# Summing the squares of two pre-norms on the tensor engine, and all residual additions of the post-norms on the vector engine

## The reference, cut to what matters

```python
x = x + rms_norm(merged @ w_out[l], norm_mix_post_g[l])     # post-norm 1, residual 1
h = rms_norm(x, norm_ffn_pre_g[l])                          # needs mean(x*x) of residual 1
f = (silu(h @ w_gate[l]) * (h @ w_up[l])) @ w_down[l]
x = x + rms_norm(f, norm_ffn_post_g[l])                     # post-norm 2, residual 2
# second block, first line:
x = x + 0.5 * swiglu(rmsnorm(x, ffn1_norm[l]), ...)         # needs mean(x*x) of residual 2
```

## Time and profile before

| | |
|---|---|
| median of 3 runs | 2029.11 us (2029.0 to 2029.81) |
| profiled execution | 2032.4 us, its span 2030.3 us |
| PE busy | 1972.8 us, 97% |
| DVE busy | 992.5 us, 49% |
| ACT busy | 761.7 us, 38% |
| POOL busy | 281.7 us, 14% |
| mean granted TensorE clock | 0.986 |

### The profile page before, as it was taken

The page is one execution under the profiler, slowest core; times in us unless marked ns, Lnnn a source line. Parts: engine busy times, 40 slices in busy tenths (PEclk is TensorE's granted clock), DMA queues, the critical chain, the costliest instruction groups (busy, mean ns, idle before and its releaser), DMA issues.

```text
span 2030.3 us, 22840 instructions
## 1 busy us (share of the span) xinstructions
PE 1972.8 (97%) x9064; PEld 1599.2 (79%) x9064; DVE 992.5 (49%) x1502; ACT 761.7 (38%) x1150; POOL 281.7 (14%) x273
## 2 busy tenths in 40 slices
PE   8989999989999999899999999999999999999997
PEld 6767788868888887688888877777887788888886
DVE  6676634374334335633433465665654454334334
ACT  5344523353223234432322355565543343223223
POOL 5121001231011012310100120120110011011012
PEclk9999999999999999999999999999899999999998
DMA  5211233423333324233333231211232233333331
GB/s 159 83 52 53 63 89 94 119 77 101 103 94 94 103 79 119 75 103 93 96 102 94 85 101 44 63 52 53 63 98 68 60 96 104 94 103 95 94 88 57
DMA packets 343404, 175.72 MB, mean 87 GB/s; under 512 B 6306, under 2 KB 343299, under 8 KB 343299
## 3 DMA queue, kind: packets, MB, share of 16 engines
q1 hardware_dynamic: 343298, 174.27, 29.7%
HBM read 172.15 MB, written 2.10 MB: 86 GB/s over the span
## 4 chain that ended last, share of the span: by engine, by line
PE 89%; DVE 5%; issue 2%; POOL 2%; ACT 1%; DMA 0%; SPq 0%; DVEq 0%; POOLq 0%; ACTq 0%
PE ps L962 27%; PE ps L966 27%; PE ps L964 26%; PE ps L1012 1%; PE ps L1021 1%; PE ps L1029 1%; PE ps L1045 1%; POOL TS L1732 1%; PE ps L982 1%; PE ps L992 1%; PE ps L1090 1%; POOL X L1758 1%; PE ps L1108 1%; PE ps L975 1%; PE ps L1033 1%
## 5 line engine op out<-in xcount | busy, mean ns | idle before, releaser
L1371 DVE TENSOR_TENSOR WL<-RAW,WH 128x1024 fp32r<-128x1024 f32 (+2 forms) x336 | 401.9, 1199 | 709.9 <-ACT WH L1147 709.6
L962 PE MATMUL ps<-HH,WH 128*128 128x512 f32 x1728 | 687.9, 398 | 7.9 <-DVE TS L1404 6.0
L966 PE MATMUL ps<-HL,WH 128*128 128x512 f32 x1728 | 679.5, 393 | 12.6 <-DVE HL L1381 12.5
L964 PE MATMUL ps<-HH,WL 128*128 128x512 f32 x1728 | 678.6, 393 | 4.0 <-DVE WL L1371 4.0
L1147 ACT ACTIVATE WH<-RAW 128x1024 fp32r<-128x1024 f32 (+2 forms) x336 | 342.3, 1021 | 543.9 <-PE ps L966 535.6
L966 PEld LDWEIGHTS ps<-HL,WH 128*128 128x128 f32 x1728 | 327.3, 189 | 87.3 <-DVE HL L1381 18.7
L962 PEld LDWEIGHTS ps<-HH,WH 128*128 128x128 f32 x1728 | 327.8, 190 | 83.9 <-DVE TS L1404 8.4
L964 PEld LDWEIGHTS ps<-HH,WL 128*128 128x128 f32 x1728 | 328.0, 190 | 74.4 <-DVE WL L1371 6.6
L962 PE MATMUL ps<-GH,WH 128*128 128x512 f32 x720 | 282.0, 392 | 0.0
L966 PE MATMUL ps<-GL,WH 128*128 128x512 f32 x720 | 280.6, 390 | 0.0
L964 PE MATMUL ps<-GH,WL 128*128 128x512 f32 x720 | 280.2, 389 | 0.0
(11 more groups left out here) (196 smaller groups left out, 1523.5 us busy)
## 6 DMA issues: line engine op xcount, KB each, us to landing
RAW<-in_ffn_w_gu SPq DMA_DIRECT2D x88, 512.0 KB, 3.8
RAW<-in_w_in SPq DMA_DIRECT2D x68, 512.0 KB, 3.9
RAW<-in_ffn_w_down SPq DMA_DIRECT2D x32, 512.0 KB, 4.0
RAW<-in_w_gate SPq DMA_DIRECT2D x22, 512.0 KB, 3.8
RAW<-in_w_up SPq DMA_DIRECT2D x22, 512.0 KB, 3.8
RAW<-in_w_out SPq DMA_DIRECT2D x16, 512.0 KB, 4.0
RAW<-in_mem_w_kv SPq DMA_DIRECT2D x16, 512.0 KB, 3.9
RAW<-in_w_down SPq DMA_DIRECT2D x16, 512.0 KB, 4.0
```

Of the source, the lines that this page charges most:

```text
L962: e.matmul(bk, wh, xh, start=k == 0, stop=False)
L964: e.matmul(bk, wl, xh, start=False, stop=False)
L966: last = e.matmul(bk, wh, xl, start=False, stop=k == kt - 1)
L1371: e.tensor_tensor(m["WL"][:, s, 0:kt, :], m["RAW"][:, n % NRAW, 0:kt, :], m["WH"][:, s, 0:kt, :].bitcast(F32), ALU.subtract).then_inc(*sg. ...
```

## The change

For generations 1 and 2 (`SUMMED`), the squares are no longer added up chunk by chunk on POOL and DVE. Each square stays in its own tile, and PE multiplies it by `onesD` into one PSUM bank that accumulates over the eight chunks (`sum_square`, f32 operands). The matmul of chunk c stands in PE's order between the first pair's matmuls of chunk c and those of chunk c+1; that of chunk 7 follows the pair. `rstd` has no matmul of its own for these two norms. All eight additions to X in each post-norm run on DVE, each right behind the scaling of the same chunk; POOL's `post` is gone, and with it the second semaphore for X.

```diff
+SUMMED = (1, 2)
...
-def x_event(gen, c):
-    return ("xp" if gen in (1, 2) and c % 2 else "x", (gen, c))
...
     def feed(self, gen, c, gcol, free):
+        key = ("n", gen)
         self.step("feed", gen, c, gcol + c, free)
-        self.square(("n", gen), c, ("X", c), T, x_event(gen, c))
+        if gen in SUMMED:
+            self.tiles.take((key, c))
+            self.step("square", key, (key, c), ("X", c), T, ("x", (gen, c)))
+        else:
+            self.square(key, c, ("X", c), T, ("x", (gen, c)))
+
+    def sum_square(self, key, c):
+        if c == 0:
+            self.bank(("stat", key))
+        self.step("sum_square", key, c)
+        self.tiles.give((key, c), ("ssq", (key, c)) if c < KD - 1 else ("stat", key))
 
     def rstd(self, key, acc, ev, ones, eps, cols=T):
-        self.bank(("stat", key))
-        self.tiles.give(acc, ("stat", key))
+        if acc is not None:
+            self.bank(("stat", key))
+            self.tiles.give(acc, ("stat", key))
...
-                if n == f == 0:
+                if n == f == 0 and gen in SUMMED:
+                    sums = iter(range(-1, KD))
+
+                    def before():
+                        c = next(sums)
+                        if c >= 0:
+                            self.sum_square(("n", gen), c)
+
+                    mg, mu = self.mtiles([sg, su], ("H", gen, 0), [bg, bu], before=before)
+                    before()
+                elif n == f == 0:
                     mg, mu = self.mtiles([sg, su], ("H", gen, 0), [bg, bu])
...
 # tensor_program
+    def sum_square(key, c):
+        g.wait_ge(*sg.at("ones", 0))
+        g.wait_ge(*sg.at("sq", (key, c)))
+        if c == 0:
+            wait_all(at.bank_free(("stat", key)))
+        e.matmul(at.bank(("stat", key)), m["onesD"], at.tile((key, c)), start=c == 0, stop=c == KD - 1).then_inc(
+            *(sg.inc("ssq", (key, c)) if c < KD - 1 else sg.inc("stat", key)))
+
     def rstd(key, acc, ev, ones, eps, cols):
+        if acc is None:
+            return
...
 # vector_program, post
-        if c % 2 == 0:
-            g.wait_ge(*sg.at("post", (gen, c)))
-            g.wait_ge(*sg.at(*x_event(gen - 1, c)))
-            e.tensor_tensor(X[:, c, :], X[:, c, :], y, ALU.add).then_inc(*sg.inc("x", (gen, c)))
+        g.wait_ge(*sg.at("post", (gen, c)))
+        g.wait_ge(*sg.at("x", (gen - 1, c)))
+        e.tensor_tensor(X[:, c, :], X[:, c, :], y, ALU.add).then_inc(*sg.inc("x", (gen, c)))
...
 # pool_program
-    def post(gen, c, t, ev, gcol):
-        if c % 2:
-            X = m["X"][:, c, :]
-            g.wait_ge(*sg.at("post", (gen, c)))
-            g.wait_ge(*sg.at(*x_event(gen - 1, c)))
-            e.tensor_tensor(X, X, at.tile(t), ALU.add).then_inc(*sg.inc("xp", (gen, c)))
```

More of the change, by code:

```diff
@@ L199, in norm @@
             self.held[gen] = True
-            self.rstd(("n", gen), ("n", gen), ("acc_last", ("n", gen)), "onesD", 0)
+            self.rstd(("n", gen), None if gen in SUMMED else ("n", gen), ("acc_last", ("n", gen)), "onesD", 0)
         return ("n", gen)
@@ L388, in post_norm @@
             self.step("post", gen, c, t, ev, gcol + c)
-            self.tiles.give(t, x_event(gen, c))
+            self.tiles.give(t, ("x", (gen, c)))
             if c:
@@ L413, in evac @@
         def evac(mt, b, mm, part=0, last=True):
-            before = ("x", (gen, mt, part - 1)) if part else x_event(gen - 1, mt)
+            before = ("x", (gen, mt, part - 1)) if part else ("x", (gen - 1, mt))
             self.step("add_x", gen, mt, b, mm, scale, before, None if last else part)
@@ L1117, in finish @@
         o.then_inc(*sg.inc("fin", 0))
-    todo = dict(gain0=gain0, gain1=gain1, turn_x=turn_x, memory_turn=memory_turn, mm=mm, rstd=rstd, turn=turn, scores=scores,
+    todo = dict(gain0=gain0, gain1=gain1, turn_x=turn_x, memory_turn=memory_turn, mm=mm, sum_square=sum_square,
+                rstd=rstd, turn=turn, scores=scores,
                 turn_probs=turn_probs, values=values, stick_map=stick_map, stick_weights=stick_weights, level=level,
@@ L1149, in feed @@
     def feed(gen, c, gcol, free):
-        g.wait_ge(*sg.at(*x_event(gen, c)))
+        g.wait_ge(*sg.at("x", (gen, c)))
         g.wait_ge(*sg.at("gain", 0 if gen == 0 else 1))
@@ L1780, in store @@
             e.tensor_tensor(y, y, m["ST"][:, 0, 0:4].unsqueeze(2).to_broadcast([P, 4, P]), ALU.mult).then_inc(*sg.inc("op", c))
-    todo = dict(first_consts=first_consts, consts=consts, square_add=square_add, scores=scores, merge=merge, gate_r=gate_r, post=post,
+    todo = dict(first_consts=first_consts, consts=consts, square_add=square_add, scores=scores, merge=merge, gate_r=gate_r,
                 prepare=prepare, k_decay=k_decay, store=store)
```

## The result

Four runs of the changed kernel gave 2013.53 us in the median (2012.71 to 2015.99), beside 2029.05 us for the kernel before (2027.14 to 2029.81, four runs). The ratio is 0.9927, interval 0.991 to 0.9944. A second measurement, with more runs of the kernel before, gave 2016.64 us (2012.63 to 2019.16, six runs) beside 2028.9 us: 0.9938, interval 0.9926 to 0.995. The forecast was 2017.2 us.

What follows compares the result with a forecast made beforehand. PE's order of work sets the time, with DVE, slowed by POOL, the bound in both post-norm stages. Gains of 5.9 and 6.0 us sum to 11.9: profiled 2032.4 to 2020.5, less 3.3 gives 2017.2 us; 8-in-10 range 2013.0 to 2021.5.

Steps and rivals of the forecast that it cites:

- DVE is the bound before, because of POOL: In both post-norm stages DVE is busy 23.50 and 22.75 us; its additions take 1.66 us beside POOL, 0.69 alone.
- the 2.05 us per chunk that was worked out: DVE in the stages without POOL: scaling 0.78, addition 0.61 and `HL` 0.66 us for each chunk.
- the four waits for `HL`: PE in the old first stage waits at chunks 1, 3, 5 and 7; one 1.81 us wait stands for all four.
- 0.87 us per f32 matmul: PE's cost for each `sum_square` at full clock; 6.1 us more PE work per stage, 12.2 in all.
- PE is the bound after, at 2.23 us per chunk: New stages: PE needs 6 x 0.227 + 0.87 us per chunk against DVE's 2.05, so PE bounds by a small margin.
- The waits for squares, banks and tiles cost nothing, and the next `WL` is in time: New stages: squares, banks and tiles cost nothing; first stage's next `WL` is done at 436.1, before PE's 437.87.
- The clock stays up: PEclk 1.00 in both stages, with no PE wait of more than 1 us.
- B: Rival: in each stage the clock still falls once, costing 1.65 us; gain 8.6, 2020.5 us; chance 0.14.
- C: Rival: low clock for most of each stage makes the kernel slower, 2038 us in a middle case, 2050 at worst; chance 0.04.
- D: Rival: DVE's additions in the stages stay slow, 3.0 us per chunk, nothing gained, within 1 us of 2029; chance 0.04.
- A: Rival: `sum_square` costs PE only 0.46 us, DVE bounds the stages, gain 15.8, 2013.3 us; chance 0.08.
- the last one, taking the stages' gain from the profiled execution over to the median: Whole kernel: profiled 2032.4 us would become 2020.5; the median, 3.3 us below the profiled run, would be 2017.2.

Runs made afterwards that it cites:

- the reduced ones: Changed kernel with squares and the matrix of 1/1024 in reduced f32 format (fp32r) for the 16 sum matmuls: 2013.8 us, ratio 0.992.
- the run with the additions alone: Kernel before with all eight additions of each post-norm on DVE, squares still summed on POOL and DVE: 2026.5 us, ratio 0.9989.
- the run with waits of 0.4 us in every 2.05 us: Changed kernel with the eight f32 matmuls of each sum all behind the pair instead of between its chunks: 2024.59 us, ratio 0.9977.

## Why the prediction was right, step by step

- *DVE is the bound before, because of POOL.* Shown: POOL's additions alone, without consumers, make the stage 24.3 us; without POOL DVE runs at the 2.05 us per chunk that was worked out. One reading of the rows was too plain: of the four waits for `HL` (chunks 1, 3, 5 and 7) three were of one kind (1.81, 1.77 and 1.80 us), and the fourth was 0.30 us, behind one of 0.65 us for ACT's `HH`. It entered no term of the sum.
- *0.87 us per f32 matmul.* 0.86 us, by itself and doubled.
- *PE is the bound after, at 2.23 us per chunk.* 2.25 us: in the stage matmuls start every 0.23 us or a little more. Stage lengths were forecast as 19.6 and 18.8 us and are 19.74 and 18.96; the sum as 11.9 us and is 11.6.
- *The waits for squares, banks and tiles cost nothing, and the next `WL` is in time.* PE's timeline shows two waits, 0.31 and 0.40 us, both in chunk 0 and as forecast, then only the short wait and restart at chunk 1, 0.27 us together, as forecast.
- *The clock stays up.* 1.00 in both stages. Rivals B and C are out, D by the 0.69 us of all sixteen additions, A by the doubled matmuls.
- *The time.* 2017.2 us against 2013.5 and 2016.6. The step that was too plain is the last one, taking the stages' gain from the profiled execution over to the median as if nothing else moved. One run holds some 28 to 42 us at low clock outside the stages, which shifts it by several us either way. Of eleven runs of the changed kernel six lie between 2012.6 and 2014.4 and four at 2018.8 or above; the first four were on the low side, by luck.
- What stays open: the medians gave 15.5 and 12.3 us, the stages 11.6. Both intervals hold 11.6 (11.4 to 18.3 and 10.1 to 15.0 us by the ratios), and three profiles of each kernel show no order in the low time; whether one or two of the extra us are the change's doing, by when the mixers' waits come, was not settled.

The forecast did not say what either half of the change is worth; the experiments give nearly all of it to the sums.

## What to carry to other kernels

A helper engine's instruction costs not only its own queue: where POOL and DVE both read two tiles of SBUF, read the durations of the DVE instructions beside it, and price a POOL addition at the microsecond that it takes from a DVE with work to do. Work put on an engine that waits for another can cost little if it fills those waits chunk by chunk (by the estimate 8 x (0.87 - 0.23) the f32 sums are 5.1 us more work for PE than the reduced ones, and they make the stage 2.0 us longer), and costs much more when the same work stands at the end (4.1 us more). Compare kernels by the length of the stage that was changed, between the same two instructions; the whole time also holds how often the clock fell elsewhere.

## What the runs showed of the hardware that was not expected

- In the run with the additions alone, POOL's additions of two 128x512 tiles and DVE's instructions with two SBUF inputs took turns: POOL's ended 1.13 to 1.15 us behind the DVE instruction that it started beside, and the DVE instruction of 0.75 us that started next ended 0.54 to 0.55 us behind POOL's. With DVE always busy that made one DVE instruction per POOL addition 1.77 us long; with POOL's addition of one tile to itself 1.53 us; with POOL's fill 0.75 us as before.
- The clock kept its full level in the run with waits of 0.4 us in every 2.05 us. In the first stage of the kernel before it fell behind waits of 1.35 and 1.81 us and again behind one of 1.77, but not behind the one of 1.80 that followed. With POOL's additions that nobody waits for it fell in the first stage (PEclk 0.93) around waits of 1.09 and 1.25 us and not in the second (1.00), where they were 0.33 and 1.24 us.
- The time at the low clock varies between runs of one program, from 20.9 to 31.7 us in the same stretch of the same kernel, and half of that, 5.4 us, is the difference in length (4.8 us) within 0.7 us.
